# Another order for the head of a decoder trunk step: shift groups and second scale group split and loaded first, first scale group unsplit behind x

## The reference, cut to what matters

```python
sc = jax.nn.silu(c)
mod = sc @ P['w_ada'][l] + P['b_ada'][l]
sh1, s1, g1, sh2, s2, g2 = jnp.split(mod[:, None, :], 6, axis=-1)
h = _rmsnorm(x, P['norm1_g'][l]) * (1 + s1) + sh1
m, na, nb, nc = _mixer(h, ...)      # z = h @ w_in is its first step
x = x + g1 * m
h = _rmsnorm(x, P['norm2_g'][l]) * (1 + s2) + sh2
x = x + g2 * _moe(h, ...)
```

## Time and profile before

| what | us |
|---|---|
| median of 3 runs (869.34, 870.34, 875.0) | 870.34 |
| the profiled execution | 873.34 |
| its span | 871.5 |
| PE busy | 837.3 (96%) |
| DVE busy | 686.0 (79%) |
| ACT busy | 465.5 (53%) |
| first product of the projection starts | 47.47 |
| second z group starts | 74.69 |

### The profile page before, as it was taken

One profiled execution on the slowest core, in us unless ns is written; L12 is line 12 of the kernel. 1 busy time (PEld: TensorE's weight loads), 2 busy tenths in 40 slices (PEclk: granted clock), 3 DMA queues, 4 the chain that ended last, 5 costly groups with the idle time before them and its releaser, 6 DMA issues.

```text
span 871.5 us, 14885 instructions
## 1 busy us (share of the span) xinstructions
PE 837.3 (96%) x5035; PEld 699.3 (80%) x5035; DVE 686.0 (79%) x942; ACT 465.5 (53%) x556; POOL 77.0 (9%) x71
## 2 busy tenths in 40 slices
PE   7899999999999999999999889999999999999994
PEld 2589999989899999899777457888888888887851
DVE  0681638878798679599438879999989999899888
ACT  4552442343422221642222457888888888888852
POOL 0002000000000000230000001000100001003750
PEclk9889999999999999999999999999999999999998
DMA  9858545445443321123671579988896899999962
GB/s 329 276 166 277 200 126 170 138 151 164 148 152 118 97 80 66 55 74 123 237 251 73 175 275 390 393 313 317 312 400 219 322 398 400 400 399 397 359 196 98
DMA packets 90997, 201.24 MB, mean 231 GB/s; under 512 B 8792, under 2 KB 13400, under 8 KB 90918
## 3 DMA queue, kind: packets, MB, share of 16 engines
q1 hardware_dynamic: 78813, 165.25, 53.8%
q0 software_dynamic: 5136, 18.42, 6.0%
q10 hardware_dynamic: 7003, 16.95, 5.2%
HBM read 182.97 MB, written 18.35 MB: 231 GB/s over the span
## 4 chain that ended last, share of the span: by engine, by line
PE 81%; DVE 9%; DMA 3%; ACT 2%; issue 2%; SPq 1%; ACTq 1%; POOL 0%; POOLq 0%; DVEq 0%
PE ps L806 31%; PE ps L657 12%; PE ps L659 12%; PE ps L658 12%; PE ps L886 3%; DVE w_lo L1592 2%; PE ps L1001 2%; DMA region_a<-in_x_prompt_dram 2%; PE ps L1123 1%; PE ps L685 1%; PE ps L686 1%; PE ps L838 1%; ACT w_hi L1148 1%; DMA region_b<-h_rows,slot_idx 1%; PE ps L1036 1%
## 5 line engine op out<-in xcount | busy, mean ns | idle before, releaser
L1592 DVE TENSOR_TENSOR w_lo<-raw,w_hi 128x1024 fp32r<-128x1024 f32 x202 | 241.5, 1225 | 100.1 <-ACT w_hi L1148 98.3
L1148 ACT ACTIVATE w_hi<-raw 128x1024 fp32r<-128x1024 f32 x202 | 207.9, 1056 | 198.2 <-PE ps L806 150.6
L657 PE MATMUL ps<-w_hi,hT_hi 128*128 128x512 f32 (+1 forms) x512 | 205.6, 401 | 3.6 <-DVE w_lo L1592 1.4
L659 PE MATMUL ps<-w_hi,hT_lo 128*128 128x512 f32 (+1 forms) x512 | 202.1, 395 | 0.0
L658 PE MATMUL ps<-w_lo,hT_hi 128*128 128x512 f32 (+1 forms) x512 | 201.5, 393 | 0.0
L806 PE MATMUL ps<-hT_hi,w_hi 128*128 128x260 f32 x768 | 156.4, 285 | 1.9 <-ACT region_b L1242 1.1
L806 PE MATMUL ps<-hT_lo,w_hi 128*128 128x260 f32 x768 | 155.0, 283 | 0.0
L806 PE MATMUL ps<-hT_hi,w_lo 128*128 128x260 f32 x768 | 154.9, 283 | 0.0
L806 PEld LDWEIGHTS ps<-hT_hi,w_hi 128*128 128x128 f32 x768 | 118.8, 189 | 5.2 <-DVE w_lo L1592 3.9
L806 PEld LDWEIGHTS ps<-hT_lo,w_hi 128*128 128x128 f32 x768 | 119.4, 190 | 0.0
L806 PEld LDWEIGHTS ps<-hT_hi,w_lo 128*128 128x128 f32 x768 | 118.9, 189 | 0.0
(11 more groups left out here) (337 smaller groups left out, 838.6 us busy)
## 6 DMA issues: line engine op xcount, KB each, us to landing
raw<-in_exp_w_dram SPq DMA_DIRECT2D x96, 512.0 KB
region_a<-in_exp_w_dram SPq DMA_DIRECT2D x80, 512.0 KB
raw<-in_w_in_dram SPq DMA_DIRECT2D x48, 512.0 KB
raw<-in_w_ada_dram SPq DMA_DIRECT2D x30, 512.0 KB
expert_rows<-region_b ACTq DMA_DIRECT2D x17, 512.0 KB, 6.3
region_b<-in_exp_w_dram SPq DMA_DIRECT2D x16, 512.0 KB
region_b<-in_w_ada_dram SPq DMA_DIRECT2D x14, 512.0 KB, 8.1
expert_rows<-region_a POOLq DMA_DIRECT2D x8, 512.0 KB, 8.4
```

What stands on the lines that cost most here:

```text
L657: pe.matmul(out, pairs[0], moving[0], start=start, stop=False)
L659: return pe.matmul(out, pairs[1], moving[0], start=False, stop=stop)
L1148: act.activation(w_hi[:, split_slot(n), :], place, ACT.Copy).then_inc(hi_done, 1)
L1592: return dve.tensor_tensor(out, whole, first.bitcast(F32), ALU.subtract)
```

## The change

The three groups 0, 1 and 3 become the split ones (`HEAD_GROUPS`), and are the first twelve quarters that SP loads. Then come x and the four quarters of group 2 (`G_WHOLE`), native. All four groups are turned ahead of the projection. The rows x_sample and the sums for the samples move from the tile `small` to `region_a`, so that `c_pad` stays whole for the native quarters; the eight multiplications by the reciprocal root are shared (ACT takes two of the four 128-row tiles). The counts of `head_running` are 24 ahead of the first quarter, 3 behind each of twelve, and 24 ahead of the turning of x, for 28 before. Behind the projection only one thing is changed: of a sum of four tiles on DVE two semaphores become one.

```diff
-G_NAT = 2
+G_WHOLE = 2
 G_HEAD = 4
 G_GAP = 2
-ITEMS = [("a", g) for g in range(G_NAT, G_HEAD)] + [("z", 0), ("z", 1)]
+HEAD_GROUPS = [g for g in range(G_HEAD) if g != G_WHOLE]
+ADA_BANK = (4, 7, 1)
+ITEMS = [("a", g) for g in HEAD_GROUPS] + [("z", 0), ("z", 1)]
 for _g in range(G_ADA - G_GAP - G_HEAD):
     ITEMS += [("a", G_HEAD + _g), ("z", 2 + _g)]
 ITEMS += [("z", _g) for _g in range(2 + G_ADA - G_GAP - G_HEAD, G_IN)]
-A_AT = {g: ITEMS.index(("a", g)) for g in range(G_NAT, G_ADA - G_GAP)}
+A_AT = {g: i for i, (kind, g) in enumerate(ITEMS) if kind == "a"}
+SPLIT_GROUPS = [g for kind, g in ITEMS if kind == "a"]
+N_NAT = 4
 Z_AT = [ITEMS.index(("z", g)) for g in range(G_IN)]
-N_HEAD = 4 * (G_HEAD - G_NAT)
+N_HEAD = 4 * len(HEAD_GROUPS)
...
-            for h in range(6):
-                native(h)
-            sp.dma_start(x_in[0:ND, 4, :], x_sample.rearrange("b t d -> (b t) d")).then_inc(x_landed[4], 16)
-            for i in range(NP // P):
-                sp.dma_start(x_in[:, i, :], x_prompt[0, i * P:(i + 1) * P, :]).then_inc(x_landed[i], 16)
-            for h in range(6, 4 * G_NAT):
-                native(h)
             for n in range(N_MIX):
-                if n == N_HEAD + 4:
+                if n == N_HEAD:
+                    sp.dma_start(x_in[0:ND, 4, :], x_sample.rearrange("b t d -> (b t) d")).then_inc(x_landed[4], 16)
+                    for i in range(NP // P):
+                        sp.dma_start(x_in[:, i, :], x_prompt[0, i * P:(i + 1) * P, :]).then_inc(x_landed[i], 16)
+                    for h in range(N_NAT):
+                        sp.dma_start(native_place(h).rearrange("p (k n) -> p k n", k=2), ada_v[:, 2 * h:2 * h + 2, G_WHOLE * COLS:(G_WHOLE + 1) * COLS]).then_inc(nat_ready[h], 16)
+                elif n == N_HEAD + RAW - 2:
                     for dst, src in state_loads:
                         sp.dma_start(dst, src).then_inc(ld_states, 16)
                 elif n == N_HEAD + RAW:
 
                     sp.wait_ge(ssq_ready, NTILE)
                     sp.wait_ge(turned, 2)
-                    sp.wait_ge(nat_used, 4 * G_NAT)
                     sp.dma_start(mod_rest, b_ada[0, 2 * D:5 * D].partition_broadcast(ND + 1)).then_inc(ld_mod, 16)
-                if n < N_APART:
-
-                    sp.wait_ge(nat_used, n + 1)
-                elif n >= RAW + N_APART:
+                if n >= N_APART + RAW:
 
                     sp.wait_ge(hi_done, n - RAW + 1)
                     sp.wait_ge(lo_done, n - RAW + 1)
                 quarter(n)
...
-            pe.wait_ge(turned_out, 1)
-            for h in range(6):
-                native_quarter(h)
-            head_running(28)
-            for h in range(6, 4 * G_NAT):
-                native_quarter(h)
+            head_running(24)
+            pe.wait_ge(cT_split, 2)
+            for n in range(N_HEAD):
+                ada_quarter(n, ADA_BANK[n // 4])
+                head_running(3)
+                if n == 5:
+                    turn_params()
+            pe.wait_ge(fold_ready, 1)
+            turn_mod(0, 0, 256)
+            turn_mod(1, 0, 292)
+            turn_mod(3, 0, 328).then_inc(modT_done, 1)
+            head_running(24)
             pe.wait_ge(xn_ready, NTILE)
             for k in range(4):
-                turn_x(k, k)
-            pe.wait_ge(cT_split, 2)
-            ada_quarter(0, 4)
-            ada_quarter(1, 4)
+                turn_x(k, X_BANK[k])
+            native_quarter(0)
+            native_quarter(1)
             for k in range(4, KD):
                 pe.wait_ge(xT_out, k - 3)
-                turn_x(k, k - 4)
-            ada_quarter(2, 4)
-            ada_quarter(3, 4)
-            pe.wait_ge(xT_out, KD)
-            turn_params()
-            ada_quarter(4, 7)
-            ada_quarter(5, 7)
-            pe.wait_ge(fold_ready, 1)
-            for g in range(3):
-                t = turn_mod(g, 0, 36 * g)
-            t.then_inc(modT_done, 1)
-            ada_quarter(6, 7)
-            ada_quarter(7, 7)
-
-
-            def z_quarter(g, q):
+                turn_x(k, X_BANK[k])
+            turn_sampled()
+            native_quarter(2)
+            native_quarter(3)
+            turn_mod(2, 0, 364).then_inc(modT_done, 1)
...
+            for n in range(N_HEAD):
+                hi(n)
...
-            hi(0)
-            hi(1)
+            for i in (2, 3):
+                act.wait_ge(x_rooted, 1)
+                act.activation(x_in[:, i, :], x_in[:, i, :], ACT.Copy, scale=sums[:, 3, i:i + 1]).then_inc(xn_ready, 1)
+            for k in range(5):
+                turned_x(k)
+            hi(12)
+            for k in range(5, KD):
+                turned_x(k)
+            act.wait_ge(nat_used, N_NAT)
+            act.activation(mod[0:ND + 1, G_WHOLE * COLS:(G_WHOLE + 1) * COLS], ps[0:ND + 1, 5, :], ACT.Copy).then_inc(nat_out, 1)
+            hi(13)
+            input_sampled(0)
             for k in range(4):
-                turned_x(k)
-            native_out(1)
-            hi(2)
-            hi(3)
-            for k in range(4, KD):
-                turned_x(k)
-            hi(4)
-            hi(5)
-            hi(6)
-            hi(7)
-            act.wait_ge(xT_out, KD)
-            input_sampled(0)
-            input_prompt(0)
-            hi(8)
-            input_prompt(1)
-            input_prompt(2)
-            input_prompt(3)
-            hi(9)
+                input_prompt(k)
             input_sampled(1)
+            hi(14)
             for k in range(4, KD):
                 input_prompt(k)
-            hi(10)
-            hi(11)
-            for n in range(N_HEAD + 4, N_HEAD + 7):
+            for n in range(N_HEAD + 3, N_HEAD + 7):
                 hi(n)
...
+            def shift_out(half):
+
+                dve.wait_ge(modT_done, 1)
+                at = 256 + 36 * half
+                dve.tensor_tensor(shiftT[:, 4 * half:4 * half + 4, :], ps[:, 0, at:at + 36].rearrange("p (k s) -> p k s", s=9),
+                                  pT[:, :, R_BIAS + half:R_BIAS + half + 1].broadcast_to([P, KW, ND + 1]), ALU.add).then_inc(shift_done, 1)
...
+            for n in range(5):
+                lo(n)
+            mod_group(0)
+            for n in range(5, 9):
+                lo(n)
+            mod_group(1)
+            params_out()
+            for n in range(9, N_HEAD):
+                lo(n)
+            mod_group(3)
+            shift_out(0)
+            shift_out(1)
+            scale_out(1)
             mean_squares()
             norm_root()
-            for t in range(NTILE):
+            dve.wait_ge(shift_done, 2)
+            dve.sem_inc(x_rooted, 1)
+            for t in (4, 0, 1):
                 dve.tensor_scalar(x_in[0:rows(t), t, :], x_in[0:rows(t), t, :], sums[0:rows(t), 3, t:t + 1], None, ALU.mult).then_inc(xn_ready, 1)
-            for n in range(5):
-                lo(n)
-            params_out()
-            mod_group(2)
-            lo(5)
-            lo(6)
-            lo(7)
+            lo(12)
+            sampled_out()
+            lo(13)
             scale_out(0)
             sampled_input(0)
+            sampled_input(1)
             prompt_sum(0)
             sampled_rest(0)
             prompt_rest(0)
-            lo(8)
-            prompt_sum(1)
-            prompt_rest(1)
-            mod_group(3)
-            for k in range(2, 4):
+            for k in range(1, 4):
                 prompt_sum(k)
                 prompt_rest(k)
-            lo(9)
-            scale_out(1)
-            sampled_input(1)
             prompt_sum(4)
             sampled_rest(1)
             prompt_rest(4)
+            lo(14)
             for k in range(5, KD):
                 prompt_sum(k)
                 prompt_rest(k)
-            lo(10)
-            lo(11)
-            lo(N_HEAD + 4)
-            lo(N_HEAD + 5)
+            for n in range(N_HEAD + 3, N_HEAD + 6):
+                lo(n)
```

126 lines of the change are left out of this document (60 added, 66 removed).

## The result

The changed kernel takes 877.41 us (median of 11 executions, 875.28 to 881.25), the kernel before 871.01 in the same rounds (868.11 to 875.08): a ratio of 1.0069, 95% interval 1.0052 to 1.0087, so 6.0 us more (4.5 to 7.6). I had predicted +3.1. The profiled execution took 881.25, 3.8 above its median; the profiled one of before, 873.34, was 2.3 above its own. Part of what follows is a matter of these two executions alone, and I say where.

A forecast was written before the change was run, and what follows sets the result against it. Bound: the head's chain from x's landing to the projection's first product, then a busy PE. First product +4.1, turning -1.0, net +3.1 on the 870.34 median: 873.4 us, range 869.5 to 879.

The forecast's parts named there:

- The projection moves as a block: Projection: PE hardly stops from 74.69 us on, so the time changes by the shift of the first z group's end.
- the native quarters come onto the path: Between x and the first product: two native quarters behind each half of x's turning, 3.5 us per pair.
- the scale waits behind `lo(13)`: Ahead of the first product: DVE's scale queues behind the split of w_in's second quarter until 48.8, turned group ready at 47.
- The moved turning of group 3: First z group: the turning inside it, 0.99 us on the path, goes; counted as -1.0.
- the clock falls sooner: Rival: PE waits 2 us for x, half clock slows turning and natives; +6 to +8, 877.5; chance 0.18.
- my own signs of being wrong: x landing outside 27.8 to 30.8, clock below 1.00 between 33 and 46, scale not waiting, or later stage absorbing 3 us.
- The first product: Start of the projection: forecast at 51.5 against 47.47 us before, +4.1.
- The twelfth quarter: Split stage: last split load, landing 4.15 behind its issue at 22.4; last `lo` done at 26.4.
- It hides, by 0.8 us: Normalization: shift path done at 29.8, ahead of x's sum of squares at 30.6.
- The unread turns: Ahead of x's turning: 24 on PE, 0.12 each, from about 29.4 to 32.2, before x at 34.1.
- my 1.89: First z group: us lost to half clock before the change, left in place by the forecast.
- the 1.07: Behind the first z group: wait of 1.07 us for ACT's issues ahead of the first output copy, taken as unchanged.

The follow-up runs named there:

- e3: Changed kernel with the split of w_in's second quarter, on ACT and DVE, moved behind the first input block; 876.68 us, ratio to before 1.0072.
- e4: Changed kernel with all twelve split quarters issued at once, without SP's waits in the head; 876.86 us, ratio to before 1.0068.
- e6: Changed kernel with 36 more unread turns on PE in the pause ahead of the first product; 874.02 us, ratio to before 1.0028.
- e8: Changed kernel with the two shift groups turned behind the tenth split quarter instead of the twelfth; 877.33 us, ratio to before 1.0070.
- e9f: e9 with 16 more unread turns on PE behind the last copy of x, ahead of the first product; 870.01 us, ratio to before 0.9971.
- e5: Changed kernel with root and multiplication of x ahead of shift and scale in DVE's order; 876.17 us, ratio to before 1.0073.
- e12: e10 with groups 0 and 1 turned behind the tenth and eleventh split quarters; 869.79 us, ratio to before 0.9990.
- e10: e9f with root before shift and scale, groups turned behind the twelfth quarter with unread turns, samples turned before x's blocks; 871.18 us, ratio to before 1.0006.
- e9: Changed kernel with ungated quarters, shift groups turned earlier, natives before x's turning, group 2 between x's halves, `lo(13)` behind the second block; 871.71 us, ratio 0.9998.
- e1: Changed kernel without the 24 unread turns ahead of the turning of x; 880.24 us, ratio to before 1.0085.
- e10b: e10 with DVE's old order, shift and scale ahead of mean and root; 871.53 us, ratio to before 1.0010.
- e2: Changed kernel with the four native quarters in place of the 24 unread turns, ahead of x's turning; 873.44 us, ratio to before 1.0026.

## Why the prediction was right, and where not

**Right: sign, mechanism, range.** The projection moves as a block, the native quarters come onto the path, the scale waits behind `lo(13)`: from the start of x's turning to the first product I had 17.4 us and it took 17.2 (37.86 to 55.07). In that stretch the mechanism held, and every size to within 0.3, 1.99 and 1.90 for the blocks and 3.54 and 3.55 for the natives. The moved turning of group 3 gave its 1.0 back. I priced the pair of semaphores behind the projection at nought, and the distance is +5.0 on both sides of it. The wait behind `lo(13)` is confirmed by e3, 1.65 us of it.

**Held by the width of the range, and partly luck.** The measured +6.0 lies above the +1 to +5 that I gave 0.62, in the band of the rival "the clock falls sooner"; what held is the range of 869.5 to 879. The sum came as near as it did because two errors offset each other: the first product was 3.5 later than I had it, and the z groups behind it gave back 1.6 more. And of my own signs of being wrong one came up in the profile: the clock was at 0.50 between 33 and 38.

**The first product, +4.1 predicted, +7.6 measured.** The missing 3.5 lie ahead of x's turning, in three terms of the sum that were mis-sized.

- The twelfth quarter: I let it land 4.15 behind its issue, by the first load, at 22.4. It landed at 25.43, 7.1 behind. The first load of an empty queue was the wrong row: by 25.4 us the queue had moved some 7.4 MB (the row under e4, added up), while twelve quarters are 6.3, so loads issued behind the quarter, those of x, had moved part of their bytes ahead of its landing. The last `lo` was done at 27.79 instead of 26.4 (+1.4). The Trainium skill, "DMA: Bandwidth & Descriptors", the section on the anatomy of one DMA, gives each DMA a fixed cost of about 2.0 us beside its bytes, fitted on DMAs issued from GpSimd; these are issued from SP. The estimate by its figures gave 21.4 for this quarter, 4.0 too early.
- "It hides, by 0.8 us": I bound the squares by the landing of x, 29.3. They are bound by ACT, which is in the split until 26.4 and then needs five times 1.24: 32.5. And the shift path ended at 33.2 instead of 29.8, since I counted the turning of one group, 1.05, where all three (24 rows, 3.26) are turned behind the last quarter, and half clock began in it. Squares and shift together: the mean square at 33.25 instead of 30.6 (+2.65, the 1.4 above within it); root and multiplication 3.7 where I had 3.5. x was ready at 36.95 instead of 34.1.
- The unread turns: I let them end at 32.2, ahead of x. At half clock they took 5.31 and ended at 37.86, 0.9 behind x.

2.85 + 0.9 - 0.2 is the 3.5.

**The first z group, -1.0 predicted, -2.6 measured for both groups.** At full clock and without a stop it takes 303.0 us from first product to last (e6). Before, it was 306.9: 1.0 of turning, 1.07 of waiting for ACT, and some 1.8 of half clock, near my 1.89. After, 304.3: 1.3 of half clock remain, 0.5 less. I had left the 1.07 in place. It went because ACT's issues ahead of the output copy took 4.4 us instead of 5.8; two of them, which load the router's biases, took 0.59 and 0.45 where they had taken 1.30 and 1.22, and in none of the three kernels in which I read them again, e6, e8 and e9f, did either take over 0.7. Why they are shorter stays open.

**The rival "the clock falls sooner"** (0.18, +6 to +8, 877.5) met both the median and the profiled execution, and its mechanism was seen in the profile, though not its trigger. I had the clock fall in a pause of PE; it fell near 31 with PE busy for 2.00 of 2 us, while it turned rows of 9 columns. The Trainium skill's page "TensorE: Matmul & The Clock Gate", section "HAM oscillation", has bursts start slow behind a wait. For the fall ahead of the projection, behind 4.57 us of idle PE, the trace and e6 agree; the fall at 31 had no longer wait than 0.45 us in the six us ahead of it. And it is not in every execution: in e3, e4, e5 and e8 the clock stayed at 1.00 through this stretch, in two of them (e5, e8) with the quarter as late as in the changed kernel. Their medians are nevertheless those of the changed kernel. So I hold that the changed kernel's median execution has no such fall either and that its profile, 3.8 above the median, overstates this part; that is argued, not shown.

**What stays open.** How the median's 6 us divide. The profiles give +5.0 at the end of the projection; behind the fall between 495 and 500, which the kernel before does not have, the expert stage is at +6 with its first product turned (524.5 and 530.6), and the last stage at +7.6 with its first product (842.1 and 849.7). The stretch ahead of the last stage varies between kernels that do not differ there (12.2 us in e12, 12.5 before, 13.6 in e10, 14.0 in the changed kernel), so I put that part down to the execution and not to the change; no run shows it.

## What to carry to other kernels

The late landing of x did not itself cost anything here, since ACT was still in the split: of a change that puts weights ahead of the activations ask which engine is free when the activations land, and what that engine still has queued. Price the whole of a moved stage, each of its groups, and price a gated load by a load in the same queue, not by the first one. A pause ahead of a long dense stage costs twice, once as a pause and once as half clock behind it: if the pause cannot go, fill it (here two lines with 36 unread turns: 1.3 us in the profile, and a median lower by 3.6, of which the rest is not explained); and where profiled executions differ in their clock, judge by medians of many.

## What the runs showed of the hardware

- The clock can differ where PE's work is the same. e8 and e9 both turned 16 rows of 9 columns in a row at 26 us, PE busy for 4.29 of 5 us before in both: in e8 the clock was 1.00 until 45, in e9 0.50 from 27 to past 40. The loads and the work behind the turning differ between the two. The stretch from 21 to 26, e8 and then e9:

```profile
21.00:26.00 5.00, 4.29 (x25) 2.69 (x23) 3.91 (x5) 1.97 (x3) 0.00 (x0) 1.00 0.91 329
...
21.00:26.00 5.00, 4.29 (x25) 2.65 (x23) 4.34 (x6) 4.25 (x6) 0.00 (x0) 1.00 1.02 402
```

- The twelfth quarter, gated by semaphores in a busy queue, landed 5.7 (e6) to 7.4 us (e5, e8) behind its issue in seven executions, and in the changed kernel the queue moved as little as 158 GB/s in a us where it otherwise moved 387.
- Half clock came back 430 us later, in a stage of narrow and native products between 475 and 515 us: 0.91 over these 40 us in e1, e10 and e10b, 0.96 in the changed kernel, e3, e4, e5, e6, e9 and e12, 1.00 in before, e2, e8 and e9f. No edit of the head is seen to go with having it or not.
